# Attention of a hybrid layer: weighing in column halves, spread inverses, key casts on GpSimd

## What is computed

```python
# mixer A: 8 heads of 64; each 64-token chunk sees itself and 8 chunks before it
sc = einsum('bqhd,bkhd->bhqk', qc, kc) * scale + bias
p = softmax(where(valid, sc, NEG_INF))
out = einsum('bhqk,bkhd->bqhd', p, vc)
# mixer B: 8 query heads on 2 key/value heads, rotary, window of 2 chunks, a sink per head
m = maximum(max(sc), sink)
p = exp(sc - m)
p = p / (sum(p) + exp(sink - m))
o = einsum('bnhgqk,bnkhd->bnqhd', p, vb)
# merge and project
x = x + (g_a * (out_a @ w_branch_a) + g_b * (out_b @ w_branch_b)) @ w_out
```

## Time and profile before

| | us |
|---|---|
| median of 3 runs | 2674.0 (2669.9 to 2674.36) |
| the profiled execution | 2678.14 |
| its span, first to last instruction | 2676.2 |
| TensorE busy | 2631.9 |
| VectorE busy | 1923.2 |
| ScalarE busy | 1159.0 |
| GpSimd busy | 252.6 |
| attention stages of both layers | 468.5 |

### The profile page before, as it was taken

The page is one execution under the profiler, slowest core; times in us unless marked ns, Lnnn a source line. Parts: engine busy times, 40 slices in busy tenths (PEclk is TensorE's granted clock), DMA queues, the critical chain, the costliest instruction groups (busy, mean ns, idle before and its releaser), DMA issues. The chain is left out here.

```text
span 2676.2 us, 36725 instructions
## 1 busy us (share of the span) xinstructions
PE 2631.9 (98%) x12920; PEld 2208.2 (83%) x12920; DVE 1923.2 (72%) x3579; ACT 1159.0 (43%) x2429; POOL 252.6 (9%) x390
## 2 busy tenths in 40 slices
PE   8999999999999999999999999999999999999998
PEld 6888888888888888888878888888888888888886
DVE  8766667644787787767996666775448887776687
ACT  6222677732533333344542227775325333333444
POOL 0000311244100000000000011112440000000000
PEclk9999999999999999999999999999999999999999
DMA  4323433253222332385423243332531332234843
GB/s 147 122 104 115 155 102 111 75 183 115 87 99 103 114 118 84 106 269 176 153 99 122 99 144 123 119 97 88 188 120 61 114 110 88 103 114 136 267 124 126
DMA packets 185236, 333.21 MB, mean 125 GB/s; under 512 B 17248, under 2 KB 62688, under 8 KB 185056
## 3 DMA queue, kind: packets, MB, share of 16 engines
q1 hardware_dynamic: 176832, 307.67, 34.6%
q10 hardware_dynamic: 8224, 23.20, 2.6%
HBM read 237.09 MB, written 92.80 MB: 123 GB/s over the span
## 5 line engine op out<-in xcount | busy, mean ns | idle before, releaser
L1203 PE MATMUL ps<-op_hi,up_hi 128*128 128x512 f32 x1232 | 479.9, 390 | 2.5 <-DVE third_sum L2781 2.5
L1205 PE MATMUL ps<-op_hi,up_lo 128*128 128x512 f32 x1232 | 479.3, 389 | 0.0
L1204 PE MATMUL ps<-op_lo,up_hi 128*128 128x512 f32 x1232 | 479.3, 389 | 0.0
L1203 PE MATMUL ps<-in_hi,up_hi 128*128 128x512 f32 x728 | 286.9, 394 | 3.3 <-DVE up_lo L2279 2.1
L1205 PE MATMUL ps<-in_hi,up_lo 128*128 128x512 f32 x728 | 285.0, 392 | 0.0
L1204 PE MATMUL ps<-in_lo,up_hi 128*128 128x512 f32 x728 | 285.0, 392 | 0.0
L1878 ACT ACTIVATE up_hi<-up_raw 128x512 fp32r<-128x512 f32 x252 | 158.0, 630 | 276.9 <-PE ps L1205 271.1
L1203 PEld LDWEIGHTS ps<-op_hi,up_hi 128*128 128x128 f32 x1232 | 231.3, 188 | 51.1 <-issue 3.3
L1205 PEld LDWEIGHTS ps<-op_hi,up_lo 128*128 128x128 f32 x1232 | 231.3, 188 | 48.3
L1204 PEld LDWEIGHTS ps<-op_lo,up_hi 128*128 128x128 f32 x1232 | 231.3, 188 | 47.6
L1173 POOL CAST w_hi<-w_raw 128x256 fp32r<-128x256 f32 x192 | 85.3, 486 | 1757.7 <-DMA w_raw<-w_lin 1199.7
(11 more groups left out here) (266 smaller groups left out, 5406.8 us busy)
## 6 DMA issues: line engine op xcount, KB each, us to landing
up_raw<-w_gu SPq DMA_DIRECT2D x42, 1024.0 KB, 5.1
act_raw<-ff_saved SPq DMA_DIRECT2D x154, 256.0 KB, 2.7
w_quarter<-w_lin SPq DMA_DIRECT2D x52, 512.0 KB, 4.4
w_raw<-w_lin SPq DMA_DIRECT2D x48, 512.0 KB, 3.7
ff_saved<-ff_block SPq DMA_DIRECT2D x88, 256.0 KB, 2.0
ff_saved<-ff_mix SPq DMA_DIRECT2D x66, 256.0 KB, 2.1
gated<-gates_saved SPq DMA_DIRECT2D x32, 512.0 KB, 4.1
stage<-in_saved SPq DMA_DIRECT2D x48, 256.0 KB, 2.8
```

Of the source, the lines that this page charges most:

```text
L1203: pe.matmul(out, w1, x1, start=first, stop=False, skip_group_check=True)
L1204: pe.matmul(out, w1, x0, start=False, stop=False, skip_group_check=True)
L1205: return pe.matmul(out, w0, x1, start=False, stop=last, skip_group_check=True)
```

## The change

- Weighing swaps its operands. The values of a head (64 columns) are stationary and the turned probabilities (128 columns) move. Head 0 writes PSUM partitions 0 to 63, head 1 partitions 64 to 127; the loop over blocks is outside, the loop over the two heads inside. The result has features on the partitions, so the transpose of each pair (`turn_pair`) and its copy (`take_pair`) go.
- The inverses, one per token, must now lie along the columns: `spread` multiplies the inverse column, broadcast to 64 columns, with the identity, one matmul per head into partition halves; ScalarE copies the result to `inverse_wide` (`take_wide`), and `take_heads` multiplies and writes into `x_sb` directly.
- Both heads are weighed together in even slots. In mixer B both units are turned together in odd slots, and one copy of 256 columns takes them. `probs` holds two B units per buffer.
- `take_heads` comes after `row_max` in VectorE's slot. `FILL_A` has new numbers with the same sums.
- The casts of mixer A's keys, all but the first two of a layer (14 per layer), go from ScalarE to GpSimd. GpSimd's program in the attention stage walks through the slots: a slot's key casts, then up to two of the eight parts of a weight split.

```diff
-FILL_A = ((3, 3, 3, 2, 2, 2, 2, 1, 1, 1, 1, 1, 1, 1, 1, 1), (1, 1, 1, 1, 1, 0, 1, 0, 1, 0, 0, 0, 1, 0, 0, 0))
+FILL_A = ((3, 3, 3, 3, 2, 3, 1, 2, 1, 1, 0, 1, 1, 1, 0, 1), (0, 1, 0, 2, 0, 1, 0, 1, 0, 1, 0, 1, 0, 1, 0, 0))
...
+def split_parts(s):
+    return [(t, part) for t in range(2, GATE_TILES) for part in range(2 * W_PARTS) if FILL_START[t - 1] + 1 + part // 2 == s]
...
+            def cast_half(L, c):
+                kind, _, half = CONV[c]
+                pool.wait_ge(*staged_when(L, c))
+                pool.tensor_copy(ka_hi[KEYS.index(kind)][:, half * HALF:(half + 1) * HALF], staged(c)).then_inc(set_or_cast, 1)
...
+                split(L, 0)
+                split(L, 1)
+                for s in range(UNITS):
+                    for c in conv_at(s, *KEYS):
+                        if is_cast(c):
+                            cast_half(L, c)
+                    for t, part in split_parts(s):
+                        split_part(L, t, part)
+                for t in range(GATE_TILES, TILES):
                     split(L, t)
...
                 for j in range(nb):
-                    mm = pe.matmul(o_ps(u)[:, e * HD:(e + 1) * HD], probs_t[u % 2][:, j * P:(j + 1) * P], values[j],
-                                   start=(j == 0), stop=(j == nb - 1))
+                    for e in range(2):
+                        rows = slice(e * HD, (e + 1) * HD)
+                        mm = pe.matmul(o_ps(u)[rows, :], blocks[j][:, rows], turns[e][:, j * P:(j + 1) * P],
+                                       start=(j == 0), stop=(j == nb - 1))
                 mm.then_inc(head_done, 1)
-            def turn_pair(L, u):
-                n = L * (UNITS // 2) + u // 2
-                pe.wait_ge(head_free, n + 1)
-                if n > 0:
-                    pe.wait_ge(pair_ready, n)
-                pe.transpose(p_ps, o_tok[:, n % 2, :], ident[:, :]).then_inc(pair_turned, 1)
+            def spread(L, u):
+                n = L * HEAD_PAIRS + u // 2
+                pe.wait_ge(inverse_ready, n + 1)
+                for e in range(2):
+                    mm = pe.matmul(wide_ps(u)[e * HD:(e + 1) * HD, :], stat[:, u % NSTAT - 1 + e, 6:7].to_broadcast([P, HD]), ident[:, :],
+                                   start=True, stop=True)
+                mm.then_inc(wide_made, 1)
...
-                    if 2 <= s < UNITS + 2:
-                        turn(L, s - 2)
-                    if 3 <= s < UNITS + 3:
+                    weighed = s >= 4 and s % 2 == 0
+                    if weighed:
                         weigh(L, s - 3)
+                    u = s - 2
+                    if 0 <= u < UNITS:
+                        if unit(u)[0] == "A":
+                            turn(L, u)
+                        elif u % 2:
+                            turn(L, u - 1)
+                            turn(L, u)
+                    if weighed:
+                        spread(L, s - 3)
                     for i, k in steps[1:]:
                         gate_step(L, i, k)
...
+            def take_wide(L, u):
+                n = L * HEAD_PAIRS + u // 2
+                act.wait_ge(wide_made, n + 1)
+                if n >= 2:
+                    act.wait_ge(head_free, n - 1)
+                act.activation(inverse_wide[:, n % 2, :], wide_ps(u), ACT.Copy).then_inc(wide_ready, 1)
...
-                for s in range(UNITS + 6):
-                    g, r = divmod(s, UNITS_PER_GROUP)
-                    if s > 6 and s % 2 == 1:
-                        take_pair(L, s - 6)
+                for s in range(UNITS + 4):
+                    if s >= 5 and s % 2 == 1:
+                        take_wide(L, s - 4)
...
-                    if 2 <= s < UNITS + 2:
+                    if 2 <= s < UNITS + 2 and (unit(s - 2)[0] == "A" or s % 2 == 1):
                         take_turned(L, s - 2)
...
-                    for c in conv_at(s, *KEYS):
-                        raise_half(L, c)
...
+                dve.wait_ge(head_done, n + 1)
+                dve.wait_ge(wide_ready, n + 1)
+                if mixer == "A":
+                    dve.tensor_tensor(x_sb[:, g, p * P:(p + 1) * P], o_ps(u), inverse_wide[:, n % 2, :], ALU.mult).then_inc(head_free, 1)
...
-                    if s % 2 == 1 and 5 <= s < UNITS + 4:
-                        take_heads(L, s - 4)
                     if s < UNITS:
                         row_max(L, s)
+                    if s % 2 == 1 and s >= 5:
+                        take_heads(L, s - 4)
```

More of the change, by code:

```diff
@@ L557, in o_ps, with wide_ps, soft, soft_last @@
             return bank(5 if mixer == "B" and u // 2 % 2 else 6)[:, 0:P]
+        def wide_ps(u):
+            mixer, _, _, _ = unit(u)
+            return bank(5 if mixer == "B" and u // 2 % 2 else 6)[:, P:2 * P]
+        def soft(u):
+            mixer, _, _, _ = unit(u)
+            first = u // NPROBS % 2 * P if mixer == "B" else 0
+            return probs[u % NPROBS][:, first:first + (P if mixer == "B" else A_COLS)]
+        def soft_last(u):
+            mixer, _, _, _ = unit(u)
+            return u - (2 * NPROBS if mixer == "B" and u % PHASE >= NPROBS else NPROBS)
         v_ps = bank(7)[:, 0:2 * P]
@@ L1173, in split @@
                     pool.tensor_copy(w_hi[slot][:, k, :], w_raw[raw][:, k, :]).then_inc(hi_made, 1)
-                for part in range(W_PARTS):
-                    k = slice(part * KT // W_PARTS, (part + 1) * KT // W_PARTS)
-                    pool.wait_ge(hi_made, W_PARTS * number + part + 1)
+                else:
+                    pool.wait_ge(hi_made, W_PARTS * number + first + 1)
                     op = pool.tensor_tensor(w_lo[slot][:, k, :], w_raw[raw][:, k, :], w_hi[slot][:, k, :], ALU.subtract)
-                op.then_inc(tile_ready, 1)
@@ L1180, in _, with split @@
-            for L in range(DEPTH):
-                for t in range(TILES):
+                    if first == W_PARTS - 1:
+                        op.then_inc(tile_ready, 1)
+            def split(L, t):
+                for part in range(2 * W_PARTS):
+                    split_part(L, t, part)
[3 more added lines that the diff above has]
+                pool.tensor_copy(ka_hi[KEYS.index(kind)][:, half * HALF:(half + 1) * HALF], staged(c)).then_inc(set_or_cast, 1)
@@ L1344, in turn @@
                 pe.wait_ge(softened, L * UNITS + u + 1)
-                if u > 0:
-                    pe.wait_ge(turned_ready, L * UNITS + u)
+                if u > 0 and (mixer == "A" or e == 0):
+                    pe.wait_ge(turned_ready, L * TURN_GROUPS + groups_turned(u - 1))
+                first = e if mixer == "B" else 0
                 for j in range(key_blocks(mixer, p)):
-                    mm = pe.transpose(t_ps[:, j * P:(j + 1) * P], probs[u % NPROBS][:, j * P:(j + 1) * P], ident[:, :])
+                    mm = pe.transpose(t_ps[:, (first + j) * P:(first + j + 1) * P], soft(u)[:, j * P:(j + 1) * P], ident[:, :])
                 mm.then_inc(turned, 1)
             def weigh(L, u):
-                mixer, g, e, p = unit(u)
+                mixer, g, _, p = unit(u)
                 nb = key_blocks(mixer, p)
+                n = L * HEAD_PAIRS + u // 2
                 if mixer == "A":
-                    values = [va[:, p + 1 - nb + j, e * HD:(e + 1) * HD] for j in range(nb)]
-                    if e == 0 and p % 2 == 0:
+                    blocks = [va[:, p + 1 - nb + j, :] for j in range(nb)]
+                    turns = probs_t
+                    if p % 2 == 0:
                         pe.wait_ge(v_ready, L * VALUES + V_PARTS * rank(CONV.index(("va", g, p // 4))) + p % 4 // 2 + 1)
@@ L1423, in attention @@
                 pe.wait_ge(in_taken, in_takes(L, IN_PAIRS - 1, 6))
-                for s in range(UNITS + 5):
+                for s in range(UNITS + 3):
                     if s < UNITS:
@@ L2541, in plain_parts, with plain_made @@
             def plain_parts(c):
-                return sum(2 if CONV[other][0] == "qa" else 1 for other in range(c) if of_kind(other) == "plain")
+                return sum(2 if CONV[other][0] == "qa" else 1 for other in range(c) if of_kind(other) == "plain" and is_cast(other) == is_cast(c))
+            def plain_made(L, c, e):
+                if is_cast(c):
+                    return set_or_cast, CONSTS_SET + L * CASTS + plain_parts(c) + 1
+                return plain_hi_ready, L * PLAIN_PARTS + plain_parts(c) + e + 1
             def lower_half(L, c, parts=(0, 1)):
```

121 lines of the change are left out of this document (59 added, 62 removed).

## The result

The changed kernel took 2700.1 us (median of four runs, 2699.3 to 2706.9), the kernel before 2672.7 in the same session (2669.9 to 2674.4). The ratio is 1.0109, interval [1.009, 1.0128]: 27 us slower, where 32 us faster was forecast. The profiled execution took 2706.9 us, with a span of 2705.1. It is the slowest of the four: TensorE's granted clock over the span was 0.994 in it and 0.997 to 0.998 in the others.

The account below looks back on a forecast made before the run. TensorE was taken to bound the kernel: -51.1 us net on its work, +5 for shape changes, -2 for ScalarE's relief and +16 for stalls gave -32 us. From the median of 2674.0 the forecast was 2642 us, range 2620 to 2708.

Parts of the forecast that it names:

- Overlap of the halves: Weighing records on TensorE: two halves share the time, 0.053 us a record instead of 0.106, saving 64.4 us.
- The rival of serial halves: Weighing and spreading on TensorE: halves run one after the other at 0.108 us a record, +47 us, 2721; chance 0.12.
- Change of shape: TensorE's queue between full width and halves: 512 changes at 0.01 us each, +5 us.
- The upper end: TensorE's array empties at each of 512 changes of shape: 0.16 us of pipeline each, 82 us.
- The base of the saving: TensorE's work before: weighing 1216 records at 0.106, 128.9 us, and 128 pair transposes at 0.108, 13.8 us.
- Stalls, +16 less 2 of relief: TensorE waiting for ScalarE's copies in A phases, +16 us; ScalarE relieved, mainly in the first B phases, -2 us.
- The walk through the pair: One A pair without gate work: odd unit's copy ends at 4.67, TensorE wants it at 4.39; 0.4 us of stall.
- the head chain: VectorE's scaling of heads waits for ScalarE's inverse copy; a slot of margin in A, alternating banks in B: 0 us.
- If the A phases do not shrink by at least 3 us each the explanation fails: Test on mixer A phases: from the second pair on near 28 us instead of 31.5, the first near 37.
- GpSimd: Key casts on GpSimd, about 1 us each, cost 0; rival of late GpSimd or SyncE +12 us, 2654, chance 0.05.
- The relief of ScalarE (-2): Fewer key casts and merged B copies on ScalarE, on the path only in the first B phases: -2 us.
- The rival with emptied arrays: Each change of shape around 128 weighings and 128 spreads empties TensorE's array: +29 us, 2703, ScalarE stalls vanish; chance 0.14.

Follow-up runs that it names:

- the experiment with 48 more runs: The changed kernel with one transpose of the turning put behind the first block product in 48 A pairs: 2715.6 us, ratio 1.0164.
- the paired one at full width: The kernel before, both units of a pair weighed in the even slot ahead of the turning, with the changed kernel's gate table: 2701.8 us, ratio 1.0106.

## Why the prediction was wrong

Two steps failed. The changes of shape stood in the sum at 5 us and measured about 50. The weighing of both units of a pair in one slot, ahead of the turning, stood in it at nothing and measured 29 at full width. Term by term:

- **Overlap of the halves (0.053 each): right**, 0.0545 within a run. The rival of serial halves is refuted, and the rule of the Trainium skill, page TensorE: Matmul & The Clock Gate, Part 3, on column groups that run side by side, agrees with this.
- **Change of shape, "I take 0.01, the nearest row": wrong, and the largest error.** The nearest row was a change of kind at one shape; it says nothing about a change of shape. The upper end, 0.16 for one change, was nearly right: 0.12 to 0.15 by the rows, 0.16 by the experiment with 48 more runs. The count was wrong as well: 512 were assumed, but in B weighing and spread stand side by side in most slots, and 380 occur. In and out of 190 runs at 0.25 to 0.30 us make 48 to 57 us instead of 5, an estimate.
- **The base of the saving, 142.7 us for weighing and pair transposes: too high.** They cost 123.0 before, since each run's first record is cheap and a transpose ahead of scores costs 0.035, not 0.108. Weighing fell by 41.5, not 64.4; the pair transposes gave 4.1, not 13.8; the spreads cost 39.2, not 27.1, as runs of four pay the changes on four records. Net -6.4 with the changes that lie inside these runs, where -51.1 was forecast, and +11.8 for the gaps of their neighbours.
- **Stalls, +16 less 2 of relief: of another kind, and by the booking of the table too small (+25.8; +13 to +14 by the finer one).** The walk through the pair put the loss on the odd unit's copy, which is there (9.4 us of waits of the weighing for `probs_t`, where before it was the turning that waited). But it never priced the step that the kernel takes on the way to halves: both units of a pair in one slot. Slots became 3.3 and 2.0 us long, for 3.0 and 1.2 us of work, while the lists of VectorE and ScalarE stayed one per slot. That, with the weighing put ahead of the turning, is 29 us at full width. Nor is the head chain free ("in A there is a slot of margin"): the heads stand ahead of a conversion, and TensorE's wait for `qb_second` is 2.0 us in the changed kernel against 1.4 in the paired one at full width.
- **Low clock: not foreseen**, 5 us of these phases in the profiled execution, behind two waits of 2.0 us; the medians do not hold it.
- **"If the A phases do not shrink by at least 3 us each the explanation fails":** they grew by 1.3 to 3.0 us, the first included. It failed.
- **GpSimd: no wait of TensorE for its casts is seen**, and none for SyncE's queue. The relief of ScalarE (-2) has the right sign here (4.5 us, with intervals that overlap) and the other in the kernel before.
- The rival with emptied arrays named 2703 us and came within 3 us, on a sum that is not the true one: it left the stalls out ("vanish behind it") and had the other terms too good. They did not vanish: part arises in the odd slots, where no weighing stands, and 9.4 us ahead of the weighing itself. That it came so near is luck.

Against the paired kernel at full width, the changed one saves 13 us on weighing and its kin and pays 17 at the neighbours and 1 in waits in the profiled executions, of which its own is 7 us above its median; the medians, 2700.1 and 2701.8, are about the same. How the 25.8 us of waits split between the engines' lists, the copies and the clock is open.

## What to carry to other kernels

When work moves between slots of a pipeline that several engines walk through by a fixed list, price the slot lengths first and alone: an edit that moves it without anything else shows the cost before the clever part is built. A saving on the bounding engine is worth what the next loop leaves of it (here turning, copy, turning, and the scores behind the row maximum), and an alternation between tile shapes has to be paid for by long runs: 0.25 to 0.30 us in and out against 0.05 saved per record is even at five to six records a run, and with the spreads at some fourteen weighing records a pair. Where nothing in the trace shows an operation, the row of a different change is not its price; keep the upper end in the forecast.

## What the runs showed of the hardware

- Column halves of f32 products overlap fully (0.0545 us a record at 128 moving columns), and a run of halves costs about 0.1 us on entry, 0.05 in its second couple, 0.10 on leaving and up to 0.06 in the first record behind it.
- A weighing record of 64 moving columns costs 0.058 us where it is the first behind a transpose and 0.112 elsewhere: two behind a transpose 0.17, ten 1.04. The price of a record depends on what stands ahead of it; why was not tested.
- TensorE's granted clock fell to 0.61 and 0.53 behind a wait of 2.0 us at the passage from A to B, which cost 1.6 and 3.4 us in two phases of the changed kernel; the paired kernels show the same behind waits of 1.4 us. Not every such wait does it: where only the last three pairs were paired, the clock fell behind the first of two waits of 1.4 us (0.59 and 0.56 from 384 to 388) and stayed at 1.00 behind the second (1712 to 1724).
